# Convolution taps, mLSTM projections and merge gates moved to earlier stages in a two-layer token-mixer and expert kernel

## The reference, cut to what matters

```python
def conformer_conv(u):                       # branch 0
    a, g = split(u)
    y = depthwise_conv(a * jax.nn.sigmoid(g), conv_w, conv_b)     # 31 taps, 512 channels
    return jax.nn.silu(layernorm(y, conv_ln_g, conv_ln_b))

# branches 1, 2, 3: bidirectional retention, bidirectional mLSTM, windowed attention
def merge(ys, gates_pre, w_branch, w_out):
    gates = jnp.split(gates_pre, N_BRANCH, axis=-1)
    acc = jax.nn.sigmoid(gates[0]) * (ys[0] @ w_branch[0])
    for i in range(1, N_BRANCH):
        acc = acc + jax.nn.sigmoid(gates[i]) * (ys[i] @ w_branch[i])
    return acc @ w_out

for l in range(2):
    x = x + ga1 * token_mixer(modulate(x, ...), modulate(ctx, ...), ...)
    x = x + ga2 * peer_ffn(modulate(x, ...), ...)      # per token 8 heads x 16 experts
    # the same for ctx in layer 0
```

## Time and profile before

| what | value |
|---|---|
| median of 3 runs | 5880.32 us (5867.57 to 5884.21) |
| the profiled execution's own time | 5877.57 us |
| its span, and what lies around it | 5875.8 us, 1.8 us |
| PE busy | 4020.7 us (68%) |
| DVE busy | 3199.4 us (54%) |
| ACT busy | 700.2 us (12%) |
| POOL busy (issuing gathers) | 2779.7 us (47%) |
| HBM traffic | 1747.5 MB, mean 297 GB/s |

### The profile page before, as it was taken

The page is one execution under the profiler, slowest core; times in us unless marked ns, Lnnn a source line. Parts: engine busy times, 40 slices in busy tenths (PEclk is TensorE's granted clock), DMA queues, the critical chain, the costliest instruction groups (busy, mean ns, idle before and its releaser), DMA issues.

```text
span 5875.8 us, 64032 instructions
## 1 busy us (share of the span) xinstructions
PE 4020.7 (68%) x23448; PEld 2399.3 (41%) x23448; DVE 3199.4 (54%) x7529; ACT 700.2 (12%) x1475; POOL 2779.7 (47%) x2602
## 2 busy tenths in 40 slices
PE   7889776777998964554456677888897544334446
PEld 5677543335565842221124434456685400000001
DVE  5421688567624885756644404645378775664430
ACT  2310122114000001000000001233200100000000
POOL 0000143566432445777776761000024677777775
PEclk9999888879999986665567888899999755555556
DMA  7545575899987989999999994121469999999999
GB/s 274 199 169 164 180 247 182 284 326 324 318 289 264 357 325 340 385 372 397 362 405 406 405 400 167 39 56 49 136 231 368 339 390 392 403 363 402 409 405 374
DMA packets 628584, 1747.51 MB, mean 297 GB/s; under 512 B 84344, under 2 KB 182520, under 8 KB 626608
## 3 DMA queue, kind: packets, MB, share of 16 engines
q0 software_dynamic: 379904, 1384.47, 62.0%
q1 hardware_dynamic: 216880, 302.74, 15.5%
q10 hardware_dynamic: 31488, 56.23, 2.7%
HBM read 1711.16 MB, written 32.07 MB: 297 GB/s over the span
## 4 chain that ended last, share of the span: by engine, by line
DMA 17%; PE 13%; issue 12%; POOL 9%; DVE 8%; ACT 1%; POOLq 0%; ACTq 0%; DVEq 0%
DMA arena<-in_peer_v,arena 11%; POOL arena L3367 9%; DMA arena<-in_peer_u,arena 5%; PE bank L850 3%; PE bank L1381 2%; DVE arena L2438 2%; PE bank L1424 2%; PE bank L1303 1%; PE bank L861 1%; PE bank L1325 1%; DVE arena L1725 1%; PE bank L1353 1%; PE bank L1255 1%; PE bank L946 1%; DVE arena L2302 0%
## 5 line engine op out<-in xcount | busy, mean ns | idle before, releaser
L3367 POOL DMA_INDIRECT arena<-in_peer_u,arena x1280 | 1431.0, 1118 | 1981.8 <-DVE arena L2328 843.6
L2438 DVE CUSTOM_DVE_ANT_0 arena<-arena 128x1024 f32<-128x1024 f32 x1280 | 1541.1, 1222 | 990.6 <-DMA arena<-in_peer_u,arena 974.6
L1424 PE MATMUL bank<-arena 128*32 128x256 f32 x10240 | 1113.0, 532 | 1234.9 <-DMA arena<-in_peer_v,arena 1229.5
L3367 POOL DMA_INDIRECT arena<-in_peer_v,arena x1280 | 1324.2, 1035 | 702.0 <-PE bank L1424 340.3
L1424 PEld LDWEIGHTS bank<-arena 128*32 128x32 f32 x10240 | 252.1, 127 | 2042.2 <-DMA arena<-in_peer_v,arena 1900.4
L850 PE MATMUL bank<-arena 128*128 128x512 f32 (+1 forms) x1600 | 637.4, 551 | 38.0 <-DVE arena L1949 10.4
L1303 PE MATMUL bank<-arena 128*128 128x256 f32 x2560 | 624.9, 405 | 21.3 <-DVE arena L2277 12.3
L1303 PEld LDWEIGHTS bank<-arena 128*128 128x128 f32 x2560 | 513.9, 204 | 134.5 <-issue 49.9
L850 PEld LDWEIGHTS bank<-arena 128*128 128x128 f32 x1600 | 317.4, 205 | 305.8 <-issue 287.7
L1381 PE MATMUL bank<-arena 128*128 128x256 f32 x1280 | 295.9, 393 | 33.4 <-DVE arena L2199 21.2
L1325 PE MATMUL bank<-arena 128*128 128x256 f32 x1280 | 289.3, 383 | 11.3 <-ACT arena L3078 4.5
(11 more groups left out here) (278 smaller groups left out, 3772.1 us busy)
## 6 DMA issues: line engine op xcount, KB each, us to landing
arena<-in_w_in SPq DMA_DIRECT2D x152, 1024.0 KB, 9.5
arena<-in_mod_w POOLq DMA_DIRECT2D x20, 2048.0 KB, 12.0
arena<-in_peer_wq SPq DMA_DIRECT2D x40, 1024.0 KB, 6.4
arena<-in_w_branch SPq DMA_DIRECT2D x30, 1024.0 KB, 5.4
arena<-in_w_out SPq DMA_DIRECT2D x20, 1024.0 KB, 7.1
arena<-in_peer_u,arena POOLq DMA_INDIRECT x1280
arena<-in_peer_v,arena POOLq DMA_INDIRECT x1280
arena<-in_w_branch SPq DMA_DIRECT2D x20, 512.0 KB, 8.0
```

The source lines that it names most:

```text
L1424: i = mm(banks[6 + g // 2][32 * j:32 * j + 32, (g % 2) * W:(g % 2 + 1) * W], G["ws"][:, g, 32 * m:32 * m + 32], G["row"][ROW_BUFFER["v", i ...
L2438: v.tensor_tensor_reduce(u, u, G["h2"][it % 2], 1.0, 0.0, ALU.mult, ALU.add, G["dots"][:, n:n + 1]).then_inc(*pr.step("dot", it, n))
L3367: fl.done(eng.indirect_dma_start(G["row"][x], None, table, bass.IndirectOffsetOnAxis(ids[:, n:n + 1], 0)), f"row_landed{x}", (kind + "_lan ...
```

## The change

It has three parts.

1. **Taps of layer 1.** In l1 the first 369 token columns (384 less the 15 that a tap reaches ahead) of all 124 taps are made in o1 already. DVE does the taps of channel groups 0 and 1 when the projections of groups 2 and 3 begin, and those of 2 and 3 at the end. 143 columns are left for the rest of l1. o1's share of expert steps is 1.6 instead of 1.0. The input rows of the last 128 tokens go to another buffer, and wait for the transposes of the block before.
2. **mLSTM projections of layer 0.** `mls1` is no stage of its own in l0 any more: the projections of head pair 1 are woven into the scan of head pair 0, with their results in other buffers. DVE's first instruction of them waits for the routing of the first expert block. The rows that the second expert block needs are loaded behind `mlss1` (at u-step 104 instead of 24).
3. **Gates of layer 0.** The six gate parts of the first 256 tokens with branches 1 to 3 are made early, three woven into retention scan 1, three into mLSTM scan 1. ACT puts a tanh of each half part into a ring of 2, and it is stored to DRAM (12 stores of 256 KB); `conv_late` reads them back on ACT's queue. The gates' weights are loaded where the gates now stand; their bytes stay the same. In `conv_late` a merge step between taps takes 1 unit (8 matmuls) instead of 3.

The core of the diff:

```diff
+def early_gates(p, f):
+    if f or p.name not in ("l0", "l1"):
+        return []
+    return merge_order(p, f) if p.name == "l1" else merge_parts(p, f)[0]
...
-    s += ["rows", "mlss0", "mls1", "mlss1", "attn"] + ["conv"] * late(p)
+    s += ["rows", "mlss0"] + ["mls1"] * (not late(p)) + ["mlss1", "attn"] + ["conv"] * late(p)
...
+def taps_ready(p):
+    return token_parts(p)[0][1] - TAPS // 2 if p is L1 else 0
...
+            def gates_made(p, parts):   
+                pn = p.name
+                for j, i_ in parts:
...
+                    names = [("gate", pn, 0, j, i_, e) for e in range(2)]
+                    for q in range(2):
+                        b = bank(("gate", pn, 0, j, i_, "pair", q))
+                        for e in range(2):
+                            w = weight_wide(names[e])
+                            for m in range(2):
+                                for k in range(QK):
+                                    i = mm(b[:, m * W:(m + 1) * W], w[:, k, (2 * q + m) * P:(2 * q + m + 1) * P],
+                                           HTk(p)[:, e * QK + k, 0:W], start=(e == m == k == 0), stop=(e == m == 1 and k == QK - 1))
...
+                        yield 7.2
...
-                        yield from first(part, 3) if what == "merge" else first(ending, 1)
+                        yield from first(part, 1) if what == "merge" else first(ending, 1)
...
-                yield from ret_scan(p, 1)
+                if late(p):
+                    yield from weave(ret_scan(p, 1), gates_made(p, early_gates(p, 0)[:3]), 0.5)
...
-                yield from mls_scan(p, 0)
-                yield from mls(p, 1)
-                yield from mls_scan(p, 1)
+                if late(p):
+                    yield from weave(mls_scan(p, 0), mls(p, 1), units(p)["mls"] / units(p)["scan"])
...
+                if late(p):
+                    yield from weave(mls_scan(p, 1), gates_made(p, early_gates(p, 0)[3:]), 0.5)
...
-            side_by_side("o1", opening(L1), side, SLOTS - LEAD, 1.0, costs)
+            side_by_side("o1", opening(L1), side, SLOTS - LEAD, 1.6, costs)
...
-            def conv_taps(p, h, part, size=8):
+            def conv_taps(p, h, part, size=8, early=False):
...
+                lo, hi = (0, taps_ready(p)) if early else (taps_ready(p), p.n)
...
-                            v.scalar_tensor_tensor(y[:, m, :], cp[:, m, j:j + p.n], tap, y[:, m, :], ALU.mult, ALU.add)\
+                            v.scalar_tensor_tensor(y[:, m, lo:hi], cp[:, m, j + lo:j + hi], tap, y[:, m, lo:hi], ALU.mult, ALU.add)\
                                 .then_inc(*mn.step())
...
-                            if n == 24:
+                            if n == (104 if it == 1 else 24):
                                 x_in(it - 1)
```

More of the change, by code:

```diff
@@ L1102, in mls @@
             def mls(p, h):
-                if h and not woven(p):
+                if h and not (woven(p) or late(p)):
                     mn.stage((f"mls{h}", p.name))
@@ L1650, in early, with gates_made @@
                 mn.stage(("gates", p.name))
-                for _ in merge_order(p, 0):
-                    for _ in range(4):
+                yield from gates_made(p, early_gates(p, 0))
+            def gates_made(p, parts):
+                for _ in parts:
+                    for _ in range(4 if p.name == "l1" else 2):
                         yield 0
@@ L1671, in conv_part @@
                 for h in range(2):
+                    if h and hi < p.n:
+                        conv_taps(p, 0, 0, TAPS, early=True)
                     for tag in ("conv_g", "conv_a"):
@@ L1960, in mls @@
                 cw, cb = par("mconv_w"), par("mconv_b")
-                if h == 0 or woven(p):
+                if h == 0 or woven(p) or late(p):
+                    if late(p) and h:
+                        eng.wait_ge(*at("experts", PC0.first + 1))
                     v.memset(M["pad"], 0.0).then_inc(*mn.step("mpad0", pn, h))
@@ L2655, in opening @@
                 yield from conv_part(p, 0)
+                yield 0
             def rest(p):
@@ L3192, in x_in @@
                         eng.wait_ge(*at("x_stored", it - 1))
+                    else:
+                        for e in ENG:
+                            eng.wait_ge(*at("end", e, ("mlss1", "l0")))
                     for j in range(COLS):
```

161 lines of the change are left out of this document (111 added, 50 removed).

## The result

The changed kernel took 5963.24 us in the median of 4 runs (5950.94 to 5985.37), the kernel before 5882.26 beside it. The ratio is 1.0149 (95% interval 1.0129 to 1.0169): slower by 81 to 88 us. The forecast was 5860.

What follows compares the result with a forecast made beforehand. No single engine was taken as the bound: DMA in most stretches, DVE or PE in some. Layer 0 -5 and layer 1 -14 sum to -19 us, from 5877.57 to 5858.6, forecast as 5860; range 5813 to 5904.

Steps and rivals of the forecast that it cites:

- Early taps at no cost in o1: Layer 1, o1: 68 us of taps on DVE, busy for 5.65 of 166 us, would be hidden.
- Layer 0: All stages from `rets1` to `conv`: changes of 42 - 13 - 16 + 65 - 15 - 68 sum to -5 us.
- 19 us hidden by the trace: o1: v-gathers slowed from 938 to 1107 ns beside taps add 19 us to POOL's 104.57 of 166, hidden.
- rival D: o1, port rule: taps block POOL, 173 of 166 us, +7 us, gathers can't catch up; total 5866, chance 0.04.
- The rest of l1, -14: Layer 1 after o1: fewer tap columns shorten PE's waits for DVE, -14 us, between 0 and -21.
- The weave, -16: Layer 0, `mlss0` with woven `mls1`: interleaving shrinks PE's idle time, 162 to 146 us, -16.
- Attention, -15: Layer 0, second part of `attn`: fewer dots on DVE and faster steps, 129 to 114 us, -15.
- `rets1` +42: Layer 0, `rets1`: more dots and routing on DVE, gates hidden under it, 42 to 84 us, +42.
- `mlss1` +65: Layer 0, `mlss1`: 50 steps instead of 31, plus gate weights and stores, 91 to 156 us, +65.
- `conv` -68: Layer 0, `conv`: six gate parts and 37 v-steps leave PE, taps end last, 252 to 184 us, -68.
- -13: Layer 0, `rows`: same 28 steps without the routing, less some new PE waiting, 105 to 92 us, -13.
- Rival B: Layer 0 scans: woven work queues behind the scan, PE waits for DVE; +28 us, 5905, chance 0.22.

Runs made afterwards that it cites:

- kernels 1 and 4 to 7: Early taps only, layer 0 as before: one piece 5910.99 us; one SBUF input, sum omitted, 5901.62; 256 columns 5902.68; parts of sixteen 5899.64; of eight 5883.01.
- kernel 3: Early taps only, layer 0 as before, issued in parts of 4 taps (8 instructions) with a full wait each: 5864.31 us, ratio 0.9972.
- Kernel 4: Early taps only, in one piece, as TENSOR_SCALAR with one SBUF input, the sum over taps left out; layer 0 as before: 5901.62 us, ratio 1.0024.
- Kernel 11: Changed kernel with only the six early gate parts, each half keeping 4 of its 16 matmuls: 5926.34 us, ratio 1.0075.
- Kernel 12: Kernel before, gates still in `conv`, but expert steps placed as with early gates: 5928.33 us, ratio 1.0083.
- kernel 9: Changed kernel with only the six early gate parts; `mls1` its own stage again, no early taps: 5925.90 us, ratio 1.0063.
- kernel 10: Only the six early gate parts, a half part yielding 0.1 instead of 7.2, so it draws no expert steps: 5921.66 us, ratio 1.0064.

## Why the prediction was wrong

*Early taps at no cost in o1* is the term that failed most. Layer 0 failed by as much in sum (-5 forecast, +50 at its end), in two terms, the weave and the attention. The prediction weighed the blocked port, priced it at 19 us hidden by the trace and, as rival D, at +7 with a chance of 0.04. It was 53 us in the changed kernel, 46 with the taps alone. The sizes were right (a tap was 0.51 us, 0.55 forecast; v-gathers rose to 1.08 to 1.24 us), but the rows came from stretches in which DVE made a full wait every 8 instructions, and the changed code has 60 without one. (The parts of 5.5 us, which the prediction calls "parts of 8 taps", are 4 taps, 8 instructions.) `conv_taps(p, 1, 0, TAPS, early=True)` has `size` as its third number, so its wait for the last instruction comes only at the first tap; this stands in the diff. Rival D's price was wrong in form as well: POOL's busy time plus the taps' (173 of 166) counts POOL as an engine with spare time. But during a block the DMA engines, which had none (share 1.00), ran dry, and all of it was lost. The Trainium skill ("SBUF — State Buffer", section "Who interferes with whom") says that the loser of the shared pair fully blocks; the changed kernel and kernels 1 and 4 to 7 agree, 28.4 us for one gather. By that section the pair is held for the whole instruction; here the gather stays out over some 50 instructions, until DVE makes a full wait, and in kernel 3, with the same instructions, no gather beside the taps takes over 1.24 us. There the measurement decides. The section ties the contention to instructions with two SBUF inputs (against a GpSimd instruction that reads SBUF), or to the modes with two ports. Kernel 4, with one input, was blocked too, but at 0.51 ns a column it may be the second of these cases, so it doesn't speak against the section.

*The rest of l1, -14:* right in mechanism, -19. The 8.0 us wait went to 1.5, and DVE's 53.39 us of 73 became 30.39 (kernel 3).

*The weave, -16:* right in sign for the weave alone (-10 in its stages), wrong in the changed kernel, +13. The prediction took 146 us, near its DMA bound of 134: 92 gathers and 4 MB at 391 GB/s, the rate of o1. The trace has 97 gathers (81 before) and a share of 0.86 of 175 us, which is 150 us of transfers, at 310 / 0.86 = 360 GB/s; the other 25 us the DMA engines idle. PE's waits for v-rows, which the prediction kept at 11.5 us in this stage, went to 39.0:

```profile
PE bank L1468 <- DMA arena<-in_peer_v,arena: 39.0, 19, 4.3
```

*Attention, -15:* wrong, +2. The prediction took DVE's and the gathers' load away and called the rest free. With 18 us less on DVE (80.82 for 98.88) PE's own chain remained: busy for 102 of 131, and waiting for ACT in between. That wait was there before as well. From 1327 to 1456 in the kernel before, and from 1447 to 1578 after:

```profile
PE bank L1255 <- ACT arena L3023: 20.9, 15, 3.6
```

```profile
PE bank L1299 <- ACT arena L3105: 22.5, 15, 4.3
```

No row of the prediction bounded this stretch by its chain.

*`rets1` +42, `mlss1` +65, `conv` -68:* 44, 66 and -75, right in mechanism. PE waited 39.5 us for the last taps in `conv`, where some 45 were forecast:

```profile
PE bank L1041 <- DVE arena L1786: 39.5, 1, 39.5
```

*The sum.* The move of gates and steps was forecast at 42 + 65 - 68 = +39 us and measured at 44 + 66 - 75 = +35. That it comes out near nothing rested on three gains beside it, -13, -16 and -15; they were -7, +13 and +2. So the prediction had the price of the move about right, and the gains that were to pay for it wrong. It took PE's idle time in the woven stage as free: PE was waiting for gathers, and what was moved in took gathers and weights with it. `conv` had been the stretch where both PE (247 of 252) and the DMA engines (0.90) were busy. Kernel 11 shows three quarters of the gates' matmuls as worth 6 us at most at the end of layer 0, and nothing in the total. Kernel 12 shows that the steps alone bring the whole loss (+85 before attention, 30 back in `conv` with the first merge), and against kernel 9 that the gates on top of them cost 37 and give back some 40. How the loss divides between steps and weights when only one is moved back is less clear: kernel 10 kept 41 of the 70 displaced gathers and 43 of the 50 us. Rival B named the right threshold (321 us for the two stages; 332 came) and the wrong place, waits for DVE; it was the v-rows. Its total of 5905 lacks the 53 us of o1.

## What to carry to other kernels

When an elementwise stream is put beside gathers that POOL issues, ask how long it runs between full waits, not only how long one instruction is (the number of instructions and the time between waits were not varied apart): a wait every 8 instructions cost 5 us here and saved 50. Before moving work to a stretch where PE idles, ask what PE waits for there; if it is a transfer, what the work carries with it (weights, or steps that a planner spreads by cost) counts nearly in full, and its matmuls little (here at most 6 us for three quarters of them). A stretch where two resources are full at once is a good one; here taking from it left the DMA engines idle.

## What the runs showed of the hardware

A POOL instruction that issues an indirect DMA can last nearly as long as a dense stream of DVE instructions: 28.44 us beside 60 of 369 columns, 22.7 beside 60 of 256, 21.08 beside 60 TENSOR_SCALAR with one SBUF input. Of the gathers that begin beside a stream two to four pass, in up to 1.24 us (0.94 alone), and the next is held. Where DVE waits for its own last instruction the hold ends, 0.8 us behind that instruction (0.1 in kernel 4). One such wait costs DVE 0.35 us. Beside parts of 8 instructions, 4.1 us, no gather was held. Why the first ones pass is open: no run varied the number of gathers in flight, or when the first comes. Open too is whether a stream with one SBUF input at 1.04 ns a column holds them.
